# One encoder layer: the attention stage walked in steps of two units instead of one

## What is computed

```python
for window, dil in PATTERNS:                 # (128, 1), (512, 4), (2048, 16)
    o, l = dilated_window_attention(q, k, v, rel_bias, window, dil)
...
s = einsum(qb, kb) * scale + bias            # bias by the true token distance
s = where(mask, s, NEG)
lse = logsumexp(s); p = exp(s - lse); o = einsum(p, vb)
...
wts = softmax(stack(lses), axis=0)           # merges the three patterns
y = concatenate([attn * silu(g_attn), four * silu(g_four)]) @ w_out
return x + y
```

## Time and profile before

| | us |
|---|---|
| median of 3 runs | 4307.66 |
| the profiled execution, its own time | 4317.7 |
| its span in the profile | 4315.9 |
| attention stage (2053 to 3712 us of the span) | 1659 |
| TensorE busy in the span | 4215.7 |
| VectorE busy | 2597.1 |
| ScalarE busy | 1688.7 |
| GpSimd busy | 848.2 |

### The profile page before, as it was taken

The page is one execution under the profiler, slowest core; times in us unless marked ns, Lnnn a source line. Parts: engine busy times, 40 slices in busy tenths (PEclk is TensorE's granted clock), DMA queues, the critical chain, the costliest instruction groups (busy, mean ns, idle before and its releaser), DMA issues. The chain is left out here.

```text
span 4315.9 us, 83865 instructions
## 1 busy us (share of the span) xinstructions
PE 4215.7 (98%) x28408; PEld 3684.1 (85%) x28408; DVE 2597.1 (60%) x7700; ACT 1688.7 (39%) x4279; POOL 848.2 (20%) x1619
## 2 busy tenths in 40 slices
PE   8999999998999999999899999999999999899999
PEld 7888888886887888888898999999989999688887
DVE  6555555555443444445666666666666766777776
ACT  4233223322111111111566565655656666433332
POOL 0000000000111111120344434444344443100000
PEclk9999999999999999999999999999999999999999
DMA  4333333337554333332445354454443533566665
GB/s 164 129 125 115 117 132 121 115 121 193 176 190 155 121 123 121 119 112 98 122 99 133 101 114 114 95 131 103 106 122 96 135 99 107 196 241 241 241 242 186
DMA packets 562981, 601.63 MB, mean 139 GB/s; under 512 B 200007, under 2 KB 438983, under 8 KB 562420
## 3 DMA queue, kind: packets, MB, share of 16 engines
q1 hardware_dynamic: 479316, 499.64, 37.3%
q0 software_dynamic: 83360, 98.05, 8.4%
HBM read 358.53 MB, written 249.08 MB: 141 GB/s over the span
## 5 line engine op out<-in xcount | busy, mean ns | idle before, releaser
L1396 ACT ACTIVATE att_p<-att_s_b,att_o 128x256 f32<-128x256 f32 (+1 forms) x1728 | 759.7, 487 | 643.9 <-DVE att_o L1451 626.1
L1341 PE MATMUL att_ps_o<-att_v,att_p_t 128*128 128x104 f32 x6528 | 798.8, 275 | 19.2 <-issue 12.3
L1341 PEld LDWEIGHTS att_ps_o<-att_v,att_p_t 128*128 128x128 f32 x6528 | 767.9, 193 | 26.3 <-issue 17.1
L1264 POOL DMA_DIRECT2D scratch_o<-att_o x864 | 505.1, 589 | 911.5 <-DVE att_o L1458 889.4
L789 PE MATMUL p_ps<-p_w_hi,p_h_hi 128*128 128x512 f32 (+1 forms) x1536 | 569.5, 371 | 14.0 <-DVE p_w_lo L966 12.6
L338 PE MATMUL p_ps<-p_w_hi,p_h_hi 128*128 128x512 f32 (+1 forms) x1536 | 568.2, 370 | 4.3 <-DVE p_w_lo L501 4.3
L338 PE MATMUL p_ps<-p_w_hi,p_h_lo 128*128 128x512 f32 (+1 forms) x1536 | 564.4, 367 | 0.0
L338 PE MATMUL p_ps<-p_w_lo,p_h_hi 128*128 128x512 f32 (+1 forms) x1536 | 564.0, 367 | 0.0
L789 PE MATMUL p_ps<-p_w_lo,p_h_hi 128*128 128x512 f32 (+1 forms) x1536 | 559.4, 364 | 0.0
L789 PE MATMUL p_ps<-p_w_hi,p_h_lo 128*128 128x512 f32 (+1 forms) x1536 | 559.1, 364 | 0.0
L1327 PE MATMUL att_ps_p<-ident,att_p 128*128 128x128 f32 x3264 | 454.3, 281 | 0.0
(11 more groups left out here) (184 smaller groups left out, 6468.4 us busy)
## 6 DMA issues: line engine op xcount, KB each, us to landing
att_v<-scratch_v SPq DMA_DIRECT2D x1056, 65.0 KB
scratch_o<-att_o POOLq DMA_DIRECT2D x864, 66.0 KB, 2.7
out_o<-scratch_o SPq DMA_DIRECT2D x144, 396.0 KB, 5.3
p_x<-x SPq DMA_DIRECT2D x48, 512.0 KB, 4.6
scratch_ht<-p_h_hi SPq DMA_DIRECT2D x48, 512.0 KB, 4.9
scratch_ht<-p_h_lo SPq DMA_DIRECT2D x48, 512.0 KB, 5.6
p_h_hi<-scratch_ht SPq DMA_DIRECT2D x48, 512.0 KB, 3.5
p_h_lo<-scratch_ht SPq DMA_DIRECT2D x48, 512.0 KB, 4.6
```

The lines of the kernel that those rows point to most:

```text
L1264: pool.dma_start(to, o[u % O][:, t, :]).then_inc(stored[u % O], 16)
L1341: ins = pe.matmul(ps_o[:, col:col + WIDE], p_t[u % 2][0:n, t, e, j, :], v[u % V][0:n, unit.chunk(at, part), e * VW:e * VW + WIDE], start=( ...
L1396: act.activation(p[u % 2][:, t, e, 0:at.w], s_b[u % 2][:, t, e, 0:at.w], ACT.Exp, bias=o[u % O][:, t, PAIR_V + e:PAIR_V + e + 1], scale=-1 ...
```

## The change

The attention's loops go over steps of two units, u = 2i and u + 1. TensorE makes the scores of u + 2 and of u + 3 in a row, then turns p of u, makes the product of u - 1, turns p of u + 1, and makes the product of u. A turn of slot u goes behind the product of u - 1, a turn of slot u + 1 behind the turning of p of u + 1. A unit's scores lie in two banks, `ps_s[2 * (u % 2) + e]`, with the two tiles side by side, so two units' scores fit in the four banks; the scores of a unit wait once for the biases of the unit two ahead of it, and count up `scored` twice instead of four times, when the second tile is done. So the bias of tile 0 waits for both tiles. There are 7 buffers `o` (5 before), 4 for sorted queries (3 before) and 3 for `p` (2 before; the third lies in the output stage's `mix[0]`, which the order prints as out_mix). The 16 turns of a next pair lie in 21 slots instead of 23, and the pieces of `w_out` begin one slot later. No matmul, bias, exponential or copy is added or taken away.

```diff
-                    slot = starts[pair - 1, 1] - 1 + 23 * i // len(todo)
-                assert slot < begin - 2
+                    slot = starts[pair - 1, 1] - 1 + 21 * i // len(todo)
+                assert slot < max(begin - 4, -2)
...
-    V, O, Q, AHEAD = 3, 5, 3, 3
+    V, O, Q, PS = 3, 7, 4, 3
...
-    slots = range(-2, N)
+    steps = range(-1, N // 2)
...
-    pieces_in = lambda slot: [i for i in range(PIECES) if last_pair + 1 + i == slot]
+    pieces_in = lambda slot: [i for i in range(PIECES) if last_pair + 2 + i == slot]
...
-        p = [sb(f"p{i}", [P, 2, 2, 2 * P]) for i in range(2)]
+        p = [sb(f"p{i}", [P, 2, 2, 2 * P]) for i in range(PS - 1)]
+        p.append(mixer.mix[0][:].rearrange("p (t e c) -> p t e c", t=2, e=2))
...
+                if u >= 2:
+                    pe.wait_ge(biased, 4 * (u - 2) + 4)
                 for t, at in enumerate(unit.tiles):
-                    if u >= 1:
-                        pe.wait_ge(biased, 4 * (u - 1) + 2 * t + 2)
...
-                            ins = pe.matmul(ps_s[2 * t + e][:, 0:at.w], x[t][half, :], at.keys(y, half),
-                                            start=(n == 0), stop=(n == 2))
-                            if n == 2:
+                            ins = pe.matmul(ps_s[2 * (u % 2) + e][:, t * 2 * P:t * 2 * P + at.w], x[t][half, :],
+                                            at.keys(y, half), start=(n == 0), stop=(n == 2))
+                            if t == 1 and n == 2:
                                 ins.then_inc(scored, 1)
...
-            for slot in slots:
-                if slot + 2 < N:
-                    score(units[slot + 2])
-                if 0 <= slot + 1 < N:
-                    turn_p(units[slot + 1])
-                for g in turns_in(slot):
-                    turn(g)
-                if slot >= 0:
-                    weigh(units[slot])
+            for i in steps:
+                u = 2 * i
+                for nr in (u + 2, u + 3):
+                    if nr < N:
+                        score(units[nr])
+                if u >= 0:
+                    turn_p(units[u])
+                    if u >= 2:
+                        weigh(units[u - 1])
+                    for g in turns_in(u):
+                        turn(g)
+                    turn_p(units[u + 1])
+                    for g in turns_in(u + 1):
+                        turn(g)
+                    weigh(units[u])
+            weigh(units[N - 1])
...
+            for i in steps:
+                u = 2 * i
+                if u + 2 < N:
+                    exponent(units[u + 2], 0)
+                if u >= 0:
+                    copy_turned(act, units[u], 0)
+                if u + 2 < N:
+                    exponent(units[u + 2], 1)
+                    exponent(units[u + 3], 0)
+                for g in turns_in(u):
                     upper(g)
+                if u >= 0:
+                    copy_turned(act, units[u + 1], 0)
+                if u + 2 < N:
+                    exponent(units[u + 3], 1)
+                for g in turns_in(u + 1):
+                    upper(g)
...
-                    dve.wait_ge(scored, 4 * u + 2 * t + e + 1)
+                    dve.wait_ge(scored, 2 * u + 2)
...
+            for i in steps:
+                u = 2 * i
+                if u >= 2:
+                    copy_o(units[u - 2])
+                if u + 2 < N:
+                    add_bias(units[u + 2], 0)
+                    add_bias(units[u + 2], 1)
+                if u >= 0:
+                    copy_turned(dve, units[u], 1)
+                if u + 2 < N:
+                    add_bias(units[u + 3], 0)
+                if u >= 2:
+                    copy_o(units[u - 1])
+                for g in turns_in(u):
+                    lower(g)
+                if u + 2 < N:
+                    add_bias(units[u + 3], 1)
+                if u >= 0:
+                    copy_turned(dve, units[u + 1], 1)
+                for g in turns_in(u + 1):
+                    lower(g)
+                for n in pieces_in(u) + pieces_in(u + 1):
+                    lower_w(n)
```

More of the change, by code:

```diff
@@ L1227, in _ @@
             sp.wait_ge(pad_done, V)
-            for slot in slots:
+            for slot in range(-2, N):
                 if slot + 2 < N:
@@ L1270, in sort_q @@
                 if i >= Q:
-                    pool.wait_ge(scored, 4 * sorted_units[i - Q] + 4)
+                    pool.wait_ge(scored, 2 * sorted_units[i - Q] + 2)
                 for n in ("q_hi", "q_lo"):
@@ L1274, in sort_q @@
                     pool.tensor_copy(to, unit.queries(core.turned[n][unit.seq])).then_inc(sorted_done, 1)
-            for u in range(AHEAD - 2):
+            for u in range(2):
                 sort_q(units[u])
-            for slot in slots:
-                if slot + AHEAD in nth_sorted:
-                    sort_q(units[slot + AHEAD])
-                if slot >= 1:
-                    store_o(units[slot - 1])
-            store_o(units[N - 1])
+            for i in steps:
+                for u in (2 * i + 4, 2 * i + 5):
+                    if u in nth_sorted:
+                        sort_q(units[u])
+                for u in (2 * i - 2, 2 * i - 1):
+                    if u >= 0:
+                        store_o(units[u])
+            for u in (N - 2, N - 1):
+                store_o(units[u])
         @block.tensor
@@ L1327, in turn_p @@
                             ins = pe.transpose(ps_p[t][0:n, (2 * e + j) * P:(2 * e + j + 1) * P],
-                                               p[u % 2][:, t, e, first:first + n], core.ident[:])
+                                               p[u % PS][:, t, e, first:first + n], core.ident[:])
                     ins.then_inc(p_turned, 1)
@@ L1401, in _ @@
                 upper(g)
-            for slot in slots:
-                if slot + 2 < N:
-                    exponent(units[slot + 2], 0)
-                if 0 <= slot + 1 < N:
-                    copy_turned(act, units[slot + 1], 0)
-                if slot + 2 < N:
-                    exponent(units[slot + 2], 1)
-                for g in turns_in(slot):
-                    upper(g)
-                if slot == last_pair + 1:
-                    act.wait_ge(scored, 4 * last_pair)
-                for i in pieces_in(slot):
-                    upper_w(i)
+            for i in steps:
[8 more added lines that the diff above has]
+                for g in turns_in(u):
+                    upper(g)
+                if u >= 0:
[4 more added lines that the diff above has]
+                    upper(g)
+                if u == last_pair + 2:
+                    act.wait_ge(scored, 2 * last_pair)
+                for n in pieces_in(u) + pieces_in(u + 1):
+                    upper_w(n)
             mixer.weights(act, 0)
@@ L1472, in _ @@
                 lower(g)
-            for slot in slots:
-                if slot >= 1:
-                    copy_o(units[slot - 1])
-                if slot + 2 < N:
-                    add_bias(units[slot + 2], 0)
-                    add_bias(units[slot + 2], 1)
-                if 0 <= slot + 1 < N:
-                    copy_turned(dve, units[slot + 1], 1)
-                for g in turns_in(slot):
-                    lower(g)
-                for i in pieces_in(slot):
-                    lower_w(i)
-            copy_o(units[N - 1])
+            for i in steps:
+                u = 2 * i
[11 more added lines that the diff above has]
+                for g in turns_in(u):
+                    lower(g)
+                if u + 2 < N:
+                    add_bias(units[u + 3], 1)
+                if u >= 0:
+                    copy_turned(dve, units[u + 1], 1)
+                for g in turns_in(u + 1):
+                    lower(g)
+                for n in pieces_in(u) + pieces_in(u + 1):
+                    lower_w(n)
+            for u in (N - 2, N - 1):
+                copy_o(units[u])
             mixer.mixed(dve, 0, 0)
```

8 lines of the change are left out of this document (4 added, 4 removed).

## The result

The changed kernel takes **4255.79 us**, median of 4 runs (4251.47 to 4257.45), against 4306.78 us for the kernel before (median of 4, 4304.42 to 4312.84): a ratio of 0.9878, 95% interval 0.9861 to 0.9895. The forecast was 4258 with a range of 4238 to 4290. The profiled execution of the changed kernel is one of these runs, 4257.45 us with a span of 4255.6. One execution of the kernel before, beside experiments 5 to 8, took 4638.6 us at a mean granted clock of 0.844 and is in no median.

A forecast was written before the change was run, and what follows sets the result against it. TensorE, busy 98% of the span, was taken as the bound. Terms of -59 - 10 - 8 + 21 + 6 = -50 us took the profiled 4317.7 to 4268; the runs' median, 10 lower, gave 4258, range 4238 to 4290.

The forecast's parts named there:

- Half of the blocks of scores lose their fee: TensorE, 215 steps with two score blocks in a row: 0.28 us saved per wide step, 0.23 per narrow, -59 us.
- the rival that it costs an entry: Seam between a step's two score blocks: 0.11 us paid 215 times, +24 us, 4282; chance 15%.
- The wait behind a turn goes: Narrow units with turns: waits for `o_copied` go because `copy_o` now stands ahead of `lower` on VectorE, -10 us.
- The last pair: Units with a piece of `w_out`: waits go that came from `lower_w` standing ahead of `copy_o`, -8 us.
- Two turns in a step: Second turn waits for the first's `lower`: 0.75 us late in 20 wide steps, 1.2 in 5 narrow, +21 us.
- Narrow steps without turns: Second product waits for `copy_o`: 0.2 us in 14 steps, 0.5 in six at the next pair's seam, +6 us.
- The loads of v: Waits for v near the narrow units: left at 6.7 us, with +7 kept for the range.
- The clock: Half clock in narrow stretches with turns: no change in the sum, -10 to +15 us in the range.
- VectorE as the bound: A step's second product waits for late `copy_o` on VectorE: 96 us more, 4354, slower than before; chance 5%.
- The increments had held TensorE: Tile 0's score blocks get shorter without increments, at most 0.05 us for each of 432 units: 4236; chance 5%.
- More waits at the turns: Half clock in all five narrow stretches and v loads twice as late: +15 + 7 us, 4280; chance 10%.

The follow-up runs named there:

- experiments 5 to 8: Changed kernel with: turn and `lower` earlier, 4258.42 us; bias loads 66 units ahead, 4260.78; both plus earlier narrow `copy_o`, 4238.31; two buffers of p, 4305.24.
- experiment 3: The kernel before with VectorE's `lower` and `lower_w` of a slot moved behind the `copy_o` that begins the next slot: 4292.93 us, ratio 0.9956.
- experiment 9: The changed kernel with the next pair's bias loads begun 42 units ahead of the pair instead of 30: 4240.42 us, ratio 0.9841.
- experiment 2: The changed kernel with four increments of `scored` in a unit again, two for each tile: 4253.66 us, ratio 0.9861.
- Experiments 9 and 10: Changed kernel, bias loads 42 units ahead: 4240.42 us; the second also has turn and `lower` earlier, and `copy_o` earlier at narrow units: 4216.61 us.

## Why the prediction was right, step by step

The mechanism was right: the fee at the border, the two turns in a step and the copy ahead of `lower` all show as told. The number was luckier than that. By the medians the difference is -51 with -50 expected, but the sum was made for the profiled execution, 4317.7 to 4268, and the profiled executions went from 4317.7 to 4257.45, which is -60. Several terms were off and partly balanced.

- **"Half of the blocks of scores lose their fee"** was right in kind and too small: 132 wide steps of the same content before and after differ by 0.34 us on average (0.35 the median), not 0.28, so about 66 us in 191 steps, not 53.5. What was mis-sized is the sum of the fee's parts. It had the entry, the first pair and the exit, and took the turning's 0.93 as the turning's own. But 0.06 of it belongs to the border; behind a product it is 0.87. The one place where a product and a turning touch showed the border, not the turning behind it, which was cut short there. A narrow step loses 0.30, not 0.23, so 7 us in 24. The seam of 0.12 held, and with it the rival that it costs an entry fell.
- **"The wait behind a turn goes"** and **"The last pair"** together were -18, and experiment 3, which makes only this move, gives -19 (4312.3 to 4292.9). That the two agree is partly luck: about 10 us of its profile are the clock, which the prediction kept as a separate term. The reading of the unit was also off. The wait of rows 6 stands at a unit without a turn, behind two units that have one: units 66 and 69 of a pair, 1.16 each, and 0.18 at units 65 and 68. That is 2.7 us in a pair and 13 in five, 10 expected, and all of it is gone. The last pair gave 6.5 by starts (8 expected): its slots 46 to 67 went from 85.0 to 74.9 us, of which 3.6 are the fee.
- **"Two turns in a step"**: +21 expected. In experiment 9, where no load of v is late, the 20 wide steps are 17.5 us over the normal one (0.88 each, 0.75 expected) and the 5 narrow ones 6.9 (1.38 each, 1.2 expected): +24. The mechanism is as told, `upper`, `lower`, then the turn; the turning between the two turns is 0.06 shorter than reckoned, and that much longer the wait.
- **"Narrow steps without turns"**: +6 expected, about 8 measured by starts. The wait where wide biases stand ahead was 0.5 in the sum and is 0.80, the ordinary one is 0.37, not 0.2, and the step behind them, at the seam to the next pair, waits 0.34 more.
- **The loads of v** were to stay at 6.7, with +7 in the range. The list says 7.7, but a wait shows there only when TensorE's records leave a gap. By starts the steps with late v, with the lower clock behind one of them, are about 12 us over what they take in experiment 9. The kernel before, read the same way, has about 16: its slots 58 to 71 take 251.0 us in five pairs, and 5 x 47.0 would be the time without late v, an estimate from the fifth pair, where 0.5 of 47.5 is a wait for v. So nothing was lost there; some 4 us were won.
- **The clock** was left at no change. Within the stage one of the two stretches at the lower level (1.2 GHz) went and one came at its very end, behind a wait of 2.5 for v. Stretches of the changed kernel, columns as in the earlier trace rows, and that wait:

```profile
2563.00:2603.00 40.00, 36.81 (x328) 34.55 (x329) 23.88 (x107) 21.00 (x56) 14.10 (x25) 0.87 0.62 148
2863.00:2903.00 40.00, 39.24 (x393) 37.12 (x393) 29.67 (x125) 26.58 (x64) 21.46 (x49) 1.00 0.45 116
...
3640.00:3650.00 10.00, 8.50 (x44) 7.95 (x44) 3.67 (x15) 2.45 (x7) 3.20 (x6) 0.66 0.29 81
```

```profile
3641.20 2.04 PE L1345 MATMUL att_ps_o<-att_v,att_p_t 128*128 128x104 f32 x8 [2.48 <-DMA att_v<-scratch_v]
```

  The new waits of up to 1.4 us at narrow turns brought none: experiment 9 has them all and, from 2073 us on, full clock throughout the stage but for that end.
- **Costs not listed** are the stage's two ends. From the last block of scores (3636.59) on the changed kernel takes 13.8 us where the kernel before took 6.9; one turning and one product more stand there now, 1.4 us, so the wait for v and the clock behind it cost +5.6. Every kernel with steps of two units waits 2.4 to 3.4 us for v there. SyncE issues the first loads of the mixing stage (3630.97 to 3633.83) ahead of the last eight loads of v; that these make v late is argued, since no run moved them. At the start, from the first scores to the end of the first product, it takes 11.69 us, 9.49 before. One block of scores more stands there, which is work done ahead, and most of the rest is no cost of the order: the clock was at its lower level for 10 us there, before for 7, and experiment 9, with the same order and 3.4 us of it, takes 10.02. Against the work done by then the start is +1.2.

Added up for the profiled stage: -66 and -7 for the borders, -13 for the waits behind turns, -6.5 for the last pair, +25 for the two turns, +8 for the narrow steps, -4 for late v and the clock behind it, +1 and +6 for the two ends. That is -57 of the 58.5 measured. Against the medians' 51.0 it is more, since the profiled execution of the kernel before was 10 over its median. The two stretches at the lower clock cost it about that much, but the other runs have no profile, so whether they lack them is not shown.

Of the rivals, **VectorE as the bound** did not come: the middle product keeps its 1.77, no more than its own length, and the second one follows its turning after 0.87. **The increments had held TensorE** is refuted by experiment 2. The semaphore tail of about 26 ns for an increment, which the Trainium skill gives (TensorE: Matmul & The Clock Gate, The cost: per-tile semaphore tail), would make 22 us for 864 of them as an estimate by that page; the medians of the two kernels differ by 2 us, the wrong way. Here the increments lie between pairs 0.12 apart, and no row shows a tail. **More waits at the turns** did not come: late v cost no more than before, and of the five stretches one was partly at the lower clock.

## What to carry to other kernels

Where the TensorE-bound loop alternates between two ways of using the array (here matmuls on half the rows and matmuls on all of them), count the borders and read their price from the starts of parts in both orders: entry, exit and the slower first instruction on either side. Batching two of a kind paid 0.35 us per block that no longer stands alone, and needs the buffers that let the rest of the loop follow (without the third buffer of p nearly all was lost). Price late loads from starts, and in both kernels alike: by the list of gaps those of v went from 6.7 to 7.7 us, by starts, with the clock behind them, from 16 to 12. And when a removed wait gives nothing, look for the next wait before dropping the edit: moves of which the larger part showed nothing alone gave 24 us once the loads of v were on time.

## What was not expected of the hardware

- Turning p (8 transposes of 128x128) takes 0.93 us behind a block of half-array matmuls and 0.87 behind a product; a product 1.87 and 1.77. The border costs the part behind it 0.06 to 0.10.
- SyncE needed up to 3.4 us to issue a load of v (median 0.6) while the bias loads were under way, and with these begun at 42 units ahead never over 1.5 in the same stretch, but up to 2.8 in the one before. The waits moved from units 60 to 62 to units 22 to 24 when the bias loads did. That the bias loads' small packets are the reason (in blocks of 128 x 16 x 8 and 128 x 16 x 4 elements) fits the place: the changed kernel moves 4096 packets of 16 bytes between 2280 and 2320 us, experiment 9 none. But no run changed the packets, so it is argued, not shown.
- Inside the stage the lower clock came with TensorE's long waits. Experiments 9 and 10, whose only late v is the last, have it only behind that one and in the stage's first 3.4 us. With two buffers of p (experiment 8) no load of v but the last is late, but waits of up to 2.0 at the turns come close together, and the clock is 0.83 to 0.96 in ten stretches of 40 us. Single waits of 0.8 to 1.4 at turns (experiment 9) did not bring it.
